# The gate-up weights of expert 14 in a fused block kernel: one 8 MiB load cut into 80 rows, six times 8 rows, and a second half

## The reference, cut to what matters

```python
def ec_moe(h, router_w, w_gu, w_down):
    cap = EC_CAPACITY_FACTOR * n // N_EXPERTS          # 2 * 256 // 16 = 32 tokens an expert
    logits = jnp.einsum('bnd,de->bne', h, router_w)
    aff = jax.nn.softmax(logits, axis=-1)
    gates, idx = lax.top_k(jnp.swapaxes(aff, 1, 2), cap)
    xs = jax.vmap(lambda hb, ib: hb[ib])(h, idx)
    def expert(args):
        xe, wgu, wd = args                              # (32, 1024), (1024, 4096), (2048, 1024)
        ga, up = jnp.split(jnp.einsum('bcd,df->bcf', xe, wgu), 2, axis=-1)
        return jnp.einsum('bcf,fd->bcd', jax.nn.silu(ga) * up, wd)
    ...                                                 # weighted by the gates and added at idx
```

## Time and profile before

| | us |
|---|---|
| median of 3 runs | 1488.92 (1487.26 to 1491.27) |
| profiled execution | 1489.12 |
| its span, first to last instruction | 1487.4 |
| TensorE busy | 1149.6 (77%) |
| VectorE busy | 464.2 (31%) |
| ScalarE busy | 401.3 (27%) |
| HBM read | 501.02 MB, 338 GB/s over the span |

### The profile page before, as it was taken

One profiled execution on the slowest core, in us unless ns is written; L12 is line 12 of the kernel. 1 busy time (PEld: TensorE's weight loads), 2 busy tenths in 40 slices (PEclk: granted clock), 3 DMA queues, 4 the chain that ended last, 5 costly groups with the idle time before them and its releaser, 6 DMA issues.

```text
span 1487.4 us, 19365 instructions
## 1 busy us (share of the span) xinstructions
PE 1149.6 (77%) x8332; PEld 755.1 (51%) x8332; DVE 464.2 (31%) x939; ACT 401.3 (27%) x898; POOL 73.6 (5%) x89
## 2 busy tenths in 40 slices
PE   9999999999998997996566556566565665565677
PEld 7888988888877875442222223223222232232234
DVE  6575777656788754010000000000000000000002
ACT  5665567555666643100000000000000000000002
POOL 0000020000035311000000000000000000000000
PEclk9999999999999998798778788787877787887799
DMA  8445546555553487999999999999999999999996
GB/s 314 170 140 200 199 170 229 210 198 199 198 186 114 157 350 306 406 434 441 427 434 436 427 433 433 434 433 438 420 446 424 427 441 425 434 431 438 424 423 286
DMA packets 29305, 503.32 MB, mean 338 GB/s; under 512 B 4130, under 2 KB 4770, under 8 KB 8100
## 3 DMA queue, kind: packets, MB, share of 16 engines
q1 hardware_dynamic: 25344, 493.43, 79.8%
q10 hardware_dynamic: 3876, 8.65, 1.6%
HBM read 501.02 MB, written 1.05 MB: 338 GB/s over the span
## 4 chain that ended last, share of the span: by engine, by line
issue 60%; PE 32%; DVE 5%; ACT 2%; POOL 1%; POOLq 0%; DVEq 0%; ACTq 0%
PE PB L374 9%; PE PB L354 5%; PE PB L355 5%; PE PB L356 5%; PE PB L375 4%; DVE SPL L1575 1%; DVE XN L1595 0%; PE PB L405 0%; POOL SP L2213 0%; PE PB L811 0%; PE PB L676 0%; PE PB L414 0%; PE PB L503 0%; ACT SPH L1041 0%; PE PB L795 0%
## 5 line engine op out<-in xcount | busy, mean ns | idle before, releaser
L913 PE MATMUL PB<-RING,XS 128*32 128x512 f32 x2048 | 294.1, 722 | 175.8 <-DMA RING<-in_wgu_dram 175.4
L913 PEld LDWEIGHTS PB<-RING,XS 128*32 128x32 f32 x2048 | 67.1, 126 | 345.5 <-issue 250.1
L945 PE MATMUL PB<-RING,HHT 128*32 128x256 f32 x2048 | 149.9, 450 | 110.5 <-DMA RING<-in_wdn_dram 109.1
L1575 DVE TENSOR_TENSOR SPL<-RAW,SPH 128x512 fp32r<-128x512 f32 x318 | 206.9, 708 | 31.3 <-ACT SPH L1041 28.7
L374 PE MATMUL PB<-XT,SPH 128*128 128x512 f32 x544 | 194.1, 401 | 0.0
L1041 ACT ACTIVATE SPH<-RAW 128x512 fp32r<-128x512 f32 x340 | 186.8, 620 | 7.2 <-DMA RAW<-in_wst_dram 3.1
L945 PEld LDWEIGHTS PB<-RING,HHT 128*32 128x32 f32 x2048 | 75.4, 128 | 169.7 <-issue 138.8
L375 PE MATMUL PB<-XT,SPL 128*128 128x256 f32 x544 | 152.3, 280 | 0.0
L1509 ACT ACTIVATE SG<-PB 128x512 f32<-128x512 f32 x16 | 9.6, 597 | 505.5 <-PE PB L913 505.5
L2103 DVE SCALAR_TENSOR_TENSOR YL<-PB,COLS,YH 128x256 fp32r<-128x256 f32 x64 | 31.0, 484 | 276.7 <-ACT YH L1523 276.7
L374 PEld LDWEIGHTS PB<-XT,SPH 128*128 128x128 f32 x544 | 102.2, 188 | 24.6
(11 more groups left out here) (393 smaller groups left out, 1575.6 us busy)
## 6 DMA issues: line engine op xcount, KB each, us to landing
RAW<-in_wst_dram SPq DMA_DIRECT2D x84, 1024.0 KB, 4.8
RING<-in_wgu_dram SPq DMA_DIRECT2D x13, 2048.0 KB, 40.2
RING<-in_wgu_dram SPq DMA_DIRECT2D x4, 4096.0 KB, 21.8
RING<-in_wgu_dram SPq DMA_DIRECT2D x14, 1024.0 KB, 8.2
RING<-in_wdn_dram SPq DMA_DIRECT2D x6, 2048.0 KB, 13.5
RING<-in_wdn_dram SPq DMA_DIRECT2D x2, 4096.0 KB, 17.9
RING<-in_wdn_dram SPq DMA_DIRECT2D x3, 1024.0 KB, 41.2
RAW<-in_wst_dram SPq DMA_DIRECT2D x4, 256.0 KB, 5.6
```

The source lines that it names most:

```text
L913: i = e.matmul(PB[b][32 * c:32 * c + 32, :], XS[x % 2][:, k, :], chunk_at(n)[:, 512 * c:512 * c + 512], start=k == 0, stop=k == KD - 1)
L945: w = e.matmul(PB[b][32 * j:32 * j + 32, 0:T], HHT[:, j, 32 * c:32 * c + 32], chunk_at(n)[:, T * (4 * (c % 2) + j):T * (4 * (c % 2) + j + ...
L1575: e.tensor_tensor(l, src, h.bitcast(F32), ALU.subtract).then_inc(*lo.up())
```

## The change

Only the load of groups 0 and 1 of expert 14, `(x, j) == (14, 0)`, is issued otherwise. The left half of the rows (group 0, 32 KB of each) is loaded by a transfer of rows 0 to 79 and six transfers of eight rows each; the right half (group 1) by one transfer of all 128 rows. All eight raise `s_ring[0]` by 16. TensorE's wait value for these two groups is raised by 16 x 7 = 112, to 304, so that it still waits for all of them.

```diff
         if e < 15:
-            return s_ring[g // 2], 16 * (e - 1 - (g < 2))
+            return s_ring[g // 2], 16 * (e - 1 - (g < 2)) + (16 * 7 if e == 14 and g < 2 else 0)
...
+        def uneven(x, j):
+
+            for a, b in ((0, 80), (80, 88), (88, 96), (96, 104), (104, 112), (112, 120), (120, 128)):
+                e.dma_start(PAIR[SLOT_OF[2 * j] // 2][a:b, 0:4 * UNIT], io["wgu"][2 * x + j][a:b, 0:4 * UNIT]).then_inc(s_ring[j], 16)
+            e.dma_start(PAIR[SLOT_OF[2 * j] // 2][:, 4 * UNIT:8 * UNIT], io["wgu"][2 * x + j][:, 4 * UNIT:8 * UNIT]).then_inc(s_ring[j], 16)
+
         for x in range(3, 15):
             for j in range(3):
                 e.wait_ge(*moe.at(("chunk", x - 1, 8 * j + 7)))
-                whole(x, j)
+                if (x, j) == (14, 0):
+                    uneven(x, j)
+                else:
+                    whole(x, j)
```

## The result

| | us |
|---|---|
| before, median of 6 runs | 1488.65 (1486.93 to 1491.27) |
| after, median of 6 runs | 1521.62 (1518.73 to 1525.03) |
| ratio | 1.0218, 95% interval 1.0206 to 1.0231 |
| after, profiled execution | 1518.73, span 1516.9 |

The change costs 33.0 us in the medians and 29.5 us between the two profiled spans (1487.4 and 1516.9; the profiled execution of the kernel after is the fastest of its six). The forecast was 18.2 us more. It was right in sign, in the cut of rows as the cause and in the place. It was too small: 1521.62 us lies above the range of 1484 to 1515.

The account below looks back on a forecast made before the run. The weight stream bounds the expert stage. Early engines need 29.2 + 6.1 = 35.3 us in place of 9.8, 25.5 more; measured from the late set's end that is +18.2: 1489.1 + 18.2 = 1507.3 us, range 1484 to 1515.

Parts of the forecast that it names:

- SP's queue: Seven more issues on SP at 0.33 us, 2.3 us in all, covered by 11 us of slack: cost nothing.
- The short transfers ride on the early eight: The 8-row transfers use the eight engines that finish first, so their delay of 25.5 us is offset by the 7.3 us gap.
- The single row: The 4 KB row of line 1531, seen near 1390.98 us on an early engine, taken to show where engine numbering begins.
- Rival 2: Short transfers on the late set at full speed: end 3.65 us later, 1492.7 us (+0.24%); chance 0.05.
- The late eight keep their pace: In the cut group, the late engines carry 13 rows instead of 16 at 1.22 us each, saving 3.65 us.
- A short transfer at 4.87 us: Eight neighbouring rows share two ways into SBUF, four engines to a way; six such transfers take 29.2 us.
- Five rows of the 80 at 1.22 us: Each early engine's five rows of the 80-row transfer run at full speed, 6.1 us together.
- The eight rows of the right half at 1.22 us: Each engine's eight rows of the whole 128-row transfer run at full speed, 9.8 us, adding no change.
- The corrections left to cancel: Staggered starts on the short transfers (end +3.6 us) and late engines writing the same ways (end +25.6 us), taken to offset.
- Rival 1: Early engines carry short transfers at 1.22 us a row, so both sets end together: 1485.7 us, down 0.23%; chance 0.32.
- Rival 3: One way for all eight rows, or late engines caught in the jam: +47 us, 1536 us; chance 0.07.
- The half-empty stretch of 10 to 18 us: Sign of the forecast: at the stream's end, eight engines have finished while the other eight still load for that long.

Follow-up runs that it names:

- the two halves: Against the kernel before, expert 14's group loaded as two transfers of 128 rows of 32 KB, left and right half; 1489.63 us, ratio 1.0000.
- the load-only run: A separate kernel that only loads, fifteen shapes of 64 KB rows, each waited for, computing nothing; eight neighbouring rows took 8.0 us a packet.

## Why the prediction was right or wrong, point by point

- *What bounds the kernel*: right. The weight stream does, the sets of eight were apart as read, and TensorE's wait for the group grew with it (9.29 to 33.29 us, forecast about 28).
- *Rows of 32 KB, one transfer more, the semaphore's value, the wait*: right, no cost (the two halves: ratio 1.0000). SP's queue: right, its eight issues took 3.4 us (1333.90 to 1337.28) and none was held.
- *The short transfers ride on the early eight, so the gap of 7.3 us may be taken off*: the step that put the time out most. The single row did ride on an early engine, but the step from there to whole sets was an assumption, named as one, and it fails for two of eight. The two late carriers end last, at 1504.3 and 1506.7 us, about 29 us later than the late set did before, and nothing comes off their delay. The early carriers, whose end the sum took for the last, end at some 1498 us, where the sum has 1495.0. So of the 11.3 us between forecast and measurement (18.2 and 29.5) the gap is 7.3. Had all eight carriers been early and the rest gone alike, the stream would have ended at about 1498 us, 21 us later than before: an estimate from these ends, not a run. Rival 2 (the wrong eight) holds for two of eight.
- *The late eight keep their pace, less 3.65 us*: the step of the mechanism that failed. The late engines without short transfers were to end 3.65 us earlier; they ended some 21 us later, at 1498. Two of them can be followed packet by packet through their 13 rows of the cut group: 1363.3 to 1399.1 and 1363.8 to 1399.9 us, 36 us where 13 x 1.22 = 15.9 was reckoned, and they began it 5 us late. The loss is common to all sixteen, down to the last packets of expert 13's weights. It didn't set the end here, because late carriers did.
- *A short transfer at 4.87 us*: high, but of the right size. In the load-only run eight neighbours took 8.0 us for 64 KB, so 4.0 us for 32 KB, between the bounds of 1.22 and 9.74. In the changed kernel the early carriers needed 20 to 22 us for their six (29.2 in the sum), 3.3 to 3.6 us each.
- *Five rows of the 80 at 1.22 us*: half of what they took. The theory of four neighbours to a way was applied to the short transfers and not to the 80 rows, though five rows an engine cross the same fours. An early carrier needed 12 us for them, 6.1 in the sum; 80 and 48 rows alone cost 17.3 us.
- *The eight rows of the right half at 1.22 us*: a term that the sum put at no change. These are whole rows again, but they shared the stream with the late engines' cut rows, and took 15 to 18 us, in place of 9.8. The three terms together made 49 us of an early carrier's time, where the sum has 45.1: that they come so near is luck, since they were off both ways.
- *The corrections left to cancel*: they didn't. The short transfers came out below 4.87 us, and what the late engines lost had no term.
- *Rival 1, the balance*: refuted for this cut. With rows 4 apart, which have no crowding among themselves, the shift still cost 13.1 us, some 3.65 of it by the two wrong carriers. A balance with eight early carriers was not tried, since none of these transfers leaves out the two.
- *Rival 3*: its second clause, late engines caught up in the jam, is what the trace shows, at some two thirds of its price (29.5 to 33.0 us for 47).
- *The range*: the upper end took five engines to a way on the short transfers alone. It lacked a case for the 80 rows, one in which everything in the stream slows, and one in which late engines are carriers; the trace shows all three. The half-empty stretch of 10 to 18 us, named as a sign, didn't come.

## What to carry to other kernels

In a stream of loads that keeps all DMA engines busy, a transfer's rows matter more than its bytes: 128 rows give every engine rows of its own, and each run of neighbouring rows short of that, tried here, made engines write into each other's. Rows 4 apart from row 0 on kept the pace in a stream, and every second row did when loaded alone. Price such a transfer by what it does to all engines, its neighbours in the queue too, and not by its own bytes: 4 MiB cut as 80 and 48 rows cost 17 us of a stream that moves 4 MiB in 9.7. And before work is moved from late engines to early ones, find out for each engine which set it is in: here one packet's evidence stood for eight engines, and two of them were late. Whether a balance would gain anything if its carriers were all early is open: what is taken from a late engine has to be written into its rows by another, and that this alone undoes the gain was argued, not shown.

## What the runs showed of the hardware that was not expected

- The rate by rows written, 64 KB rows, one transfer at a time, from issue to next issue: 128 rows 22.0 us, rows 80 to 127 26.5 us, rows 0 to 79 27.4 us, every second row (64) 12.5 us, rows 0 to 63 23.1 us. Rows 0 to 95 took 4.9 us a packet.
- In a full stream one engine that writes outside its own rows slows itself and one more to 4.8 us a 64 KB packet; two slow all sixteen to 5.2 us, if each writes into the rows of another engine. Two in the rows of one slow just the engines concerned (13 of 264 packets).
- The early and the late engines are not the two halves of the numbering: of the eight that carry an 8-row transfer, six were early and two late.
- A short transfer in its engines' own rows costs nothing beyond its bytes: 50.7 us where 41.2 and 9.7 make 50.9.
